# One encoder layer on one core: twelve of GpSimd's quarter sums in the first token block, probabilities transposed ahead of the weighing, first values loaded through GpSimd

## The chip, the cores and the metric

The kernel runs on one core of a Trainium2 chip. The core has a matrix engine (TensorE, PE in the profile; PEld is its weight load), VectorE (DVE), ScalarE (ACT), GpSimd (POOL) and SyncE (SP), which only issues transfers and handles semaphores. All engines run their own instruction streams and meet at semaphores. The metric is device time of one execution in microseconds, from launch to end.

## The reference, cut to what matters

One layer over 2560 tokens (a prompt of 2048 and a sample of 512), model width 1024, float32. The order of the computation is the order of the kernel:

```
h = rmsnorm(x, norm1_w)
proj = h @ w_in                       # q, k, v, z, xBC, dt
q = rmsnorm(q) * 64 ** -0.5;  k = rmsnorm(k)          # per head of 64
s = q . k_window + bias               # window of 8 rows x 16 columns on a grid 64 wide
p = softmax(s);  att = p @ v_window   # 8 heads
xBC = silu(depthwise_conv(xBC, 5 taps))
ssm = state-space mixer(z, xBC, dt)   # forward and backward scan
x = x + concat(att, ssm) @ w_out
x = x + (silu(h2 @ w_gate) * (h2 @ w_up)) @ w_down    # h2 = rmsnorm(x)
```

## The kernel before, in words

Six phases run one after the other, with a barrier of all engines between them: the input projection (tiles named i_), the attention (a_), the state-space mixer (s_), the output projection (o_), the upward (u_) and the downward (d_) half of the feed-forward part. The change touches the first two.

**Matrix products** are made of three passes over numbers split into a high and a low part (lines 65 to 67), so each weight tile i_raw becomes i_w_hi (ScalarE, L332) and i_w_lo (VectorE, L460).

**Input projection.** Five token blocks of 512 tokens each go through twelve slots s = 0 to 11 of weights. Slots 0 to 3 make xBC, 4 and 5 make z, 6 and 7 make v, 8 and 9 make q, 10 and 11 make k. Four accumulators acc[:, u] hold the four rows of 128 tokens. TensorE may start an accumulator again only when the last result in it has been taken: in slot 8 it waits for the copy of v by VectorE (L524), in slot 10 for q. The result q is scaled by VectorE (L509) and then multiplied in place by its gain by GpSimd (L630), and only GpSimd's multiplication raises the semaphore ev_ready that slot 10 waits for. At the end of a block GpSimd also makes three of the four low parts of the next block's input (L570); VectorE makes the fourth (L480). TensorE transposes the next block's input in slots 8, 9, 10 and 11 (L662).

The depthwise convolution of one token block runs a block later, in slots 4 to 7: ScalarE does the first tap (L370), VectorE the four others (L492, named taps here). In the first block (number 0) there is no earlier block, so it has no taps. The last block (number 4) does its own taps and those of block 3.

Beside this, GpSimd prepares operands for the feed-forward part, 33 of them: it loads four quarters of a weight matrix into i_ops (two transfers of 512 KB), forms four sums or differences in four instructions (L604, L605, L607, L609, and the same on L612 to L617 for the last eleven), and stores 1 MB (L620). These are the quarter sums. i_ops has two buffers: before sum n is made, the load for n + 1 is issued, and that load waits until the store of sum n - 1 has landed:

```
for n in range(OPS * tb, min(OPS * (tb + 1), 3 * FP)):
    if n + 1 < 3 * FP:
        load_ops(n + 1)
    make_ops(n)
for u in range(TT):
    pool.wait_ge(q_scaled[u], tb + 1)
    ...                               # L630, the gain of q
```

OPS is 7 and FP is 11, so blocks 0 to 3 do seven sums each and block 4 does five. In GpSimd's order they all stand ahead of the gain of q of their block.

**Attention.** Eight heads, each in 20 tiles a of 128 queries, with 3, 4, 4, 3 and 2 groups of 128 keys in the five bands of four tiles. In step a each engine does work for several tiles: TensorE makes the scores of tile a (L1143, L1144), weighs the values of tile a - 3 (L1164) and transposes the probabilities of tile a - 2 (L1152). VectorE adds the bias and takes the maximum of tile a (L964), inverts the sum of a - 1 (L979) and scales the probabilities of a - 1 if a - 1 is even (L984); GpSimd scales them if it is odd (L906). ScalarE copies the transposed probabilities of a - 2 out to a_probT (L1066), which has two buffers, and then takes the exponential of a (L1059). The q and k of the following head are prepared in between: split by ScalarE (L1039, L1040) and GpSimd (L897, L900), transposed by TensorE (L1114 to L1123), copied out by VectorE and ScalarE. At the start of the phase the same preparation is done for head 0 alone, GpSimd issues the loads of four mask blocks (L927, 480 KB each), and SP issues, in this order: q and k of head 0 in five groups, the bias of head 0 (8 transfers), the values of head 0 (L865, 16 transfers of 80 KB), then q and k (L851, L852), bias and values of head 1.

Of the kernel before, what the change touches and what calls it, by code (L numbers as in the profile page):

```python
# [23 lines left out]
HEAD = 64  # L24
# [45 lines left out]
def in_proj_phase(nc, x, w_in, cols, qk_w, bias_pad, copies, ident_dram, w_ffn, w_down, q_s, k_s, v_s, z_s, dtT, xbcT, xcT,  # L70
# [19 lines left out]
    HALO = D_CONV // 2  # L90
    CB = 4
    LAST_CONVS = (3, 3, 2, 2, 3, 1, 2, 0)
    OPS = 7

    with ExitStack() as ctx:
        def sb(name, shape, dt=F32):
# [469 lines left out]
        def _(pool):  # L566
# [53 lines left out]
                pool.dma_start(dst, ops[:, buf, 4:8]).then_inc(ops_stored[buf], 16)  # L620

            def token_block(tb, more, conv):
                for n in range(OPS * tb, min(OPS * (tb + 1), 3 * FP)):
                    if n + 1 < 3 * FP:
                        load_ops(n + 1)
                    make_ops(n)
                for u in range(TT):
                    pool.wait_ge(q_scaled[u], tb + 1)
                    view = ev[:, u].rearrange("p (h d) -> p h d", h=HEADS)
                    pool.tensor_tensor(view, view, q_gain[:].unsqueeze(1).broadcast_to([P, HEADS, HEAD]), ALU.mult) \  # L630
                        .then_inc(ev_ready[u], 1)
                if more:
                    for u in range(TT - 1):
                        h_low(tb + 1, u)
# [79 lines left out]
def attention_phase(nc, q_s, k_s, v_s, copies, masks, ident_dram, mixT):  # L714
# [27 lines left out]
    with ExitStack() as ctx:  # L742
# [36 lines left out]
        qk_loaded = some("qk_loaded", 2)  # L779
        first_loaded = some("first_loaded", BANDS)  # L780
        v_loaded = some("v_loaded", 2)
        bias_loaded = some("bias_loaded", 2)

        hi_made = sem("hi_made")
# [57 lines left out]
        def _(sp):  # L842
# [29 lines left out]
                if g == 0:  # L872
                    sp.dma_start(ident[:], ident_dram).then_inc(const_loaded, 16)
            load_bias((0, 0))
            load_v((0, 0))
            load_qk((0, 1))
            load_bias((0, 1))
            load_v((0, 1))
# [11 lines left out]
        def _(pool):  # L890
# [18 lines left out]
            def pair(i, first, last):  # L909
                for par in range(2):  # L910
# [3 lines left out]
                    for a in range(NT):  # L914
# [3 lines left out]
                        if ahead and a in at:  # L918
                            split_low(following(head), at[a])

            for g in range(BANDS):
                split_low((0, 0), g)
                if g in (1, 3):

                    i = g // 2
                    for side, which in ((qb[i], 0), (kb[i], 1)):
                        pool.dma_start(side[MASK0:MASK0 + MASKS], masks[:, which].bitcast(F32R)) \  # L927
                            .then_inc(masks_set[i], 16)
# [179 lines left out]
        def _(pe):  # L1108
# [46 lines left out]
            def weigh(head, a):  # L1155

                G, b, c, par = NT * number(head) + a, a // COLT, a % COLT, head[1]
                if a == 0:
                    pe.wait_ge(v_loaded[par], 16 * 16 * (head[0] + 1))
                if c == 0:  # L1160
                    wait(pe, o_out, BANDS * number(head) + b)
                pe.wait_ge(p_out, G + 1)
                for j in range(COUNT[b]):
                    last = pe.matmul(ps_o[HEAD * par:HEAD * (par + 1), c], v[:, par, c * KG + FIRST[b] + j],  # L1164
                                     probT[:, a % 2, j], start=j == 0, stop=j == COUNT[b] - 1)
                last.then_inc(weighed, 1)

            def pair(i, first, last):
                for par in range(2):
                    head = (i, par)  # L1170
                    ahead = not (last and par == 1)
                    at = FIRST_GROUP_AT if first and par == 0 else GROUP_AT
                    for a in range(NT):
                        scores(head, a)
                        late = behind(head, a, LAG_PV, first)
                        if late:
                            weigh(*late)
                        late = behind(head, a, LAG_TURN, first)
                        if late:
                            turn_p(*late)  # L1180
                        if ahead and a - 2 in at:
                            turn_q(following(head), at[a - 2])
                        if ahead and a - 3 in at:
                            turn_k(following(head), at[a - 3])
# [1624 lines left out]
```

## Time and profile before

| What | Value |
|---|---|
| Median of 3 runs | 3399.82 us (3389.86 to 3411.44) |
| The profiled execution | 3394.09 us, its span 3392.3 us |
| TensorE busy | 3157.7 us, 93% |
| VectorE, ScalarE, GpSimd busy | 1968.5, 1410.6, 703.6 us |
| Granted TensorE clock, mean | 0.970 |
| Input projection | 0 to 788 us |
| Attention | 789 to 1178 us |

The span runs from the first to the last instruction; 1.8 us of the profiled time lie outside it. Times in a row of the trace count from the start of the span. A clock of 1.00 is 2.4 GHz, 0.50 is 1.2 GHz.

### The profile page before, as it was taken

The page shows a single profiled execution, that of the slowest core. Times are in us where ns is not written, and L with a number is a line of the kernel's source. Part 1 is how long each engine was busy: PE and PEld are TensorE (multiplying, and loading weights), DVE is VectorE, ACT ScalarE, POOL GpSimd, SP SyncE. Part 2 cuts the span into 40 slices and gives each one's busy share as a digit, 9 for nine tenths or more (in the row PEclk, how much of TensorE's full clock was granted, in tenths as well). Part 3 has the DMA queues.
Part 4 walks back from the last instruction along what each step waited for, and adds up shares of the span by engine and source line. Part 5 has one row for each costly group of instructions (what it writes and reads, how often), then busy time and mean ns, then how long its engine had stood idle before and what let it go on. Part 6 is the DMA issues. An engine that isn't in the chain of part 4 may idle for free. (4 is left out here: it accounts for less than half of the span.)

```text
span 3392.3 us, 47727 instructions
## 1 busy us (share of the span) xinstructions
PE 3157.7 (93%) x15896; PEld 2674.9 (79%) x15896; DVE 1968.5 (58%) x3011; ACT 1410.6 (42%) x2711; POOL 703.6 (21%) x706
## 2 busy tenths in 40 slices
PE   7999999996999868869979999999999998999999
PEld 6877877774777645658868999999999997888887
DVE  3446556374666556964446555755576664555655
ACT  3334434344676536852224333432343333434443
POOL 5353534412333235832210000000000000000000
PEclk9999999998999978989989999999999998999999
DMA  8685959577333022346765545655575556566875
GB/s 275 227 295 211 332 176 347 185 249 139 80 79 76 28 81 73 93 149 211 220 212 172 159 151 162 225 157 154 154 227 175 173 175 212 211 216 241 279 243 211
DMA packets 458543, 630.37 MB, mean 186 GB/s; under 512 B 133168, under 2 KB 271968, under 8 KB 453984
## 3 DMA queue, kind: packets, MB, share of 16 engines
q1 hardware_dynamic: 431936, 522.72, 48.8%
q0 software_dynamic: 23600, 100.80, 8.4%
q10 hardware_dynamic: 2880, 5.24, 0.4%
q8 instruction: 70, 1.15, 0.1%
q14 instruction: 57, 0.47, 0.0%
HBM read 451.45 MB, written 177.75 MB: 185 GB/s over the span
## 5 line engine op out<-in xcount | busy, mean ns | idle before, releaser
L65 PE MATMUL u_acc<-u_h_hi,u_w_hi 128*128 128x448 f32 (+1 forms) x1848 | 657.1, 356 | 25.2 <-DVE u_h_lo L2378 19.9
L66 PE MATMUL u_acc<-u_h_lo,u_w_hi 128*128 128x448 f32 (+1 forms) x1848 | 656.5, 355 | 0.0
L67 PE MATMUL u_acc<-u_h_hi,u_w_lo 128*128 128x448 f32 (+1 forms) x1848 | 656.5, 355 | 0.0
L65 PEld LDWEIGHTS u_acc<-u_h_hi,u_w_hi 128*128 128x128 f32 x1848 | 347.7, 188 | 45.2 <-DVE u_w_lo L2366 22.8
L66 PEld LDWEIGHTS u_acc<-u_h_lo,u_w_hi 128*128 128x128 f32 x1848 | 347.7, 188 | 18.4
L67 PEld LDWEIGHTS u_acc<-u_h_hi,u_w_lo 128*128 128x128 f32 x1848 | 347.6, 188 | 18.4
L2622 ACT CAST d_hi<-d_raw 128x896 fp32r<-128x896 f32 (+1 forms) x231 | 224.2, 980 | 279.8 <-DMA d_raw<-hid_ops 151.2
L460 DVE TENSOR_TENSOR i_w_lo<-i_raw,i_w_hi 128x2048 fp32r<-128x2048 f32 x60 | 155.3, 2589 | 305.6 <-ACT i_w_hi L332 305.6
L2643 DVE TENSOR_TENSOR d_lo<-d_raw,d_hi 128x896 fp32r<-128x896 f32 (+1 forms) x231 | 252.0, 1133 | 113.3 <-ACT d_hi L2622 108.4
L65 PE MATMUL d_acc<-d_hi 128*128 128x512 f32 x770 | 301.8, 392 | 17.1 <-DVE d_lo L2643 12.8
L66 PE MATMUL d_acc<-d_lo,d_hi 128*128 128x512 f32 x770 | 301.3, 391 | 0.0
L67 PE MATMUL d_acc<-d_hi,d_lo 128*128 128x512 f32 x770 | 301.3, 391 | 0.0
L65 PE MATMUL i_acc<-i_w_hi,i_h_hi 128*128 128x512 f32 x640 | 257.7, 403 | 10.4 <-DVE i_ev L524 10.4
L66 PE MATMUL i_acc<-i_w_lo,i_h_hi 128*128 128x512 f32 x640 | 255.8, 400 | 0.0
L67 PE MATMUL i_acc<-i_w_hi,i_h_lo 128*128 128x512 f32 x640 | 255.7, 400 | 0.0
L2321 ACT ACTIVATE u_gate<-u_gate 128x448 f32<-128x448 f32 (+1 forms) x99 | 55.6, 562 | 401.5 <-DVE u_gate L2421 204.9
L2366 DVE TENSOR_TENSOR u_w_lo<-u_w_lo,u_w_hi 128x512 fp32r<-128x512 f32 x264 | 180.6, 685 | 50.7 <-ACT u_w_hi L2306 43.4
L65 PEld LDWEIGHTS d_acc<-d_hi 128*128 128x128 f32 x770 | 145.7, 189 | 48.4 <-DVE d_lo L2643 13.2
L1164 PE MATMUL a_ps_o<-a_probT,a_v 128*64 128x128 f32 x1024 | 148.0, 283 | 34.2 <-ACT a_probT L1066 19.6
L332 ACT CAST i_w_hi<-i_raw 128x2048 fp32r<-128x2048 f32 x60 | 114.4, 1907 | 151.0 <-PE i_acc L67 150.3
L1164 PEld LDWEIGHTS a_ps_o<-a_probT,a_v 128*64 128x64 f32 x1024 | 109.1, 138 | 85.2 <-ACT a_probT L1066 49.1
L2306 ACT CAST u_w_hi<-u_w_lo 128x512 fp32r<-128x512 f32 x264 | 152.7, 616 | 43.5 <-DMA u_w_lo<-w_ops 43.5
(265 smaller groups left out, 6072.3 us busy)
## 6 DMA issues: line engine op xcount, KB each, us to landing
u_w_lo<-w_ops SPq DMA_DIRECT2D x264, 256.0 KB, 2.9
i_raw<-w_in_dram SPq DMA_DIRECT2D x60, 1024.0 KB, 6.5
u_w_raw<-w_ffn_dram SPq DMA_DIRECT2D x198, 256.0 KB, 3.2
d_raw<-wd_ops SPq DMA_DIRECT2D x132, 256.0 KB, 5.5
d_raw<-hid_ops SPq DMA_DIRECT2D x154, 192.0 KB, 6.1
d_raw<-w_down_dram SPq DMA_DIRECT2D x99, 256.0 KB, 5.7
i_ops<-w_ffn_dram POOLq DMA_DIRECT2D x44, 512.0 KB, 6.5
w_ops<-i_ops POOLq DMA_DIRECT2D x22, 1024.0 KB, 6.3
```

The source lines that it names most:

```text
L65: pe.matmul(out, w_hi, x_hi, start=first, stop=False, skip_group_check=resumed)
L66: pe.matmul(out, w_hi, x_lo, start=False, stop=False, skip_group_check=resumed)
L67: return pe.matmul(out, w_lo, x_hi, start=False, stop=last, skip_group_check=resumed)
L332: act.copy(w_hi[:, par], raw[:, par]).then_inc(slot_hi_done[par], 1)
L460: dve.tensor_tensor(w_lo[:, par], raw[:, par], w_hi[:, par].bitcast(F32), ALU.subtract) \
L1164: last = pe.matmul(ps_o[HEAD * par:HEAD * (par + 1), c], v[:, par, c * KG + FIRST[b] + j], probT[:, a % 2, j], start=j == 0, stop=j == COU ...
L2306: act.copy(w_hi[:, n], weights(n)).then_inc(w_hi_done, 1)
L2321: act.activation(gate[:, c, 0:n], gate[:, c, 0:n], ACT.Silu).then_inc(silu_done, 1)
L2366: dve.tensor_tensor(w_lo[:, n], weights(n), w_hi[:, n].bitcast(F32), ALU.subtract) \
L2622: act.copy(hi[:, r, 0:TB + w], raw[:, r, 0:TB + w]).then_inc(hi_done, 1)
L2643: dve.tensor_tensor(lo[:, r, 0:TB + w], raw[:, r, 0:TB + w], hi[:, r, 0:TB + w].bitcast(F32), ALU.subtract) \
```

## The change

Three edits. The table OPS_AT gives blocks 0 to 4 of the input projection 12, 5, 5, 5 and 6 sums in place of 7, 7, 7, 7 and 5; the total stays 33. The values of head 0 are issued by GpSimd, ahead of its first splits, and not by SP; they have a semaphore of their own, and the counts of the old one are lowered for even heads. In each attention step the transposition of tile a - 2 stands ahead of the weighing of tile a - 3.

```diff
-    OPS = 7
+    OPS_AT = (0, 12, 17, 22, 27, 33)
...
             def token_block(tb, more, conv):
-                for n in range(OPS * tb, min(OPS * (tb + 1), 3 * FP)):
+                for n in range(OPS_AT[tb], OPS_AT[tb + 1]):
                     if n + 1 < 3 * FP:
                         load_ops(n + 1)
                     make_ops(n)
...
+        first_v_loaded = sem("first_v_loaded")
...
             load_bias((0, 0))
-            load_v((0, 0))
             load_qk((0, 1))
...
+            v_src = v_s.rearrange("(m r c) d -> r c m d", r=4, c=GRID_W)
+            for c in range(COLT):
+                for r in range(4):
+                    pool.dma_start(v[32 * r:32 * r + 32, 0, c * KG:(c + 1) * KG], v_src[r, COL[c]:COL[c] + 32, :, 0:HEAD]) \
+                        .then_inc(first_v_loaded, 16)
             for g in range(BANDS):
                 split_low((0, 0), g)
...
                 if a == 0:
-                    pe.wait_ge(v_loaded[par], 16 * 16 * (head[0] + 1))
+                    if isinstance(head[0], int) and head == (0, 0):
+                        pe.wait_ge(first_v_loaded, 16 * 16)
+                    else:
+                        pe.wait_ge(v_loaded[par], 16 * 16 * (head[0] + par))
...
                         scores(head, a)
+                        late = behind(head, a, LAG_TURN, first)
+                        if late:
+                            turn_p(*late)
                         late = behind(head, a, LAG_PV, first)
                         if late:
                             weigh(*late)
-                        late = behind(head, a, LAG_TURN, first)
-                        if late:
-                            turn_p(*late)
```

GpSimd at the end of block 0 of the input projection, before: one quarter sum (the seventh), then the gain of q and the low parts.

```order
L604 TENSOR_TENSOR i_ops<-i_ops 128x512
L605 TENSOR_TENSOR i_ops<-i_ops 128x512
L607 TENSOR_TENSOR i_ops<-i_ops 128x512
L609 TENSOR_TENSOR i_ops<-i_ops 128x512
L620 DMA w_ops<-i_ops 128x2048
L630 TENSOR_TENSOR i_ev<-i_ev,i_q_gain 128x512 x4
L570 TENSOR_TENSOR i_h_lo<-i_h_f,i_h_hi 128x8x128 x3
```

The same place as a difference; the first of the five sums that are added is shown, and the four others stand between it and the gain of q.

```order
 L609 TENSOR_TENSOR i_ops<-i_ops 128x512
 L620 DMA w_ops<-i_ops 128x2048
+L577 DMA i_ops<-w_ffn_dram 128x1024
+L579 DMA i_ops<-w_ffn_dram 128x1024
+L604 TENSOR_TENSOR i_ops<-i_ops 128x512
+L605 TENSOR_TENSOR i_ops<-i_ops 128x512
+L607 TENSOR_TENSOR i_ops<-i_ops 128x512
+L609 TENSOR_TENSOR i_ops<-i_ops 128x512
+L620 DMA w_ops<-i_ops 128x2048
```

Five such groups of seven rows now stand ahead of L630 and L570 of block 0 on GpSimd.

TensorE in an attention step with four groups of keys, before.

```order
L1143 MATMUL a_ps_s<-a_ka,a_qa 128x512
L1144 MATMUL a_ps_s<-a_kb,a_qb 128x512
L1164 MATMUL a_ps_o<-a_probT,a_v 64x128 x4
L1152 MATMUL a_ps_p<-a_ident,a_prob 128x128 x4
```

And the same step now (the line numbers are those of the changed kernel; L1148 and L1149 are the scores, L1157 the transposition, L1172 the weighing).

```order
L1148 MATMUL a_ps_s<-a_ka,a_qa 128x512
L1149 MATMUL a_ps_s<-a_kb,a_qb 128x512
L1157 MATMUL a_ps_p<-a_ident,a_prob 128x128 x4
L1172 MATMUL a_ps_o<-a_probT,a_v 64x128 x4
```

The last two groups have changed places, and so have the waits in front of them.

GpSimd at the start of the attention, now; before, the first row was not there.

```order
L924 DMA a_v<-v_s 32x10x64 x16
L897 TENSOR_TENSOR a_q_st<-a_q_raw,a_q_st 128x4x64
L900 TENSOR_TENSOR a_k_st<-a_k_raw,a_k_st 128x4x64
L897 TENSOR_TENSOR a_q_st<-a_q_raw,a_q_st 128x4x64
L900 TENSOR_TENSOR a_k_st<-a_k_raw,a_k_st 128x4x64
L932 DMA a_qb<-masks_dram 48x2560
L932 DMA a_kb<-masks_dram 48x2560
```

All of GpSimd's work of the start, the splits that TensorE waits for and the mask loads, now stands behind the sixteen issues.

## Rows read from the trace of the kernel before

**Rows 1.** The page: the span.

```profile
span 3392.3 us, 47727 instructions
```

**Rows 2.** Time line of GpSimd, block 0: start us, us, what, [idle before <-releaser].

```profile
93.18 0.53 POOL L577 DMA_DIRECT2D i_ops<-w_ffn_dram  x1 [3.89 <-DMA w_ops<-i_ops]
...
108.74 0.53 POOL L577 DMA_DIRECT2D i_ops<-w_ffn_dram  x1 [8.45 <-DMA w_ops<-i_ops]
...
120.13 0.53 POOL L577 DMA_DIRECT2D i_ops<-w_ffn_dram  x1 [4.26 <-DMA w_ops<-i_ops]
...
126.67 0.58 POOL L620 DMA_DIRECT2D w_ops<-i_ops  x1 [0.30 <-POOL i_ops L609]
143.29 1.28 POOL L630 TENSOR_TENSOR i_ev<-i_ev,i_q_gain 128x512 f32<-128x512 f32 x1 [16.04 <-DVE i_ev L509]
```

**Rows 3.** Time line of TensorE: the transposition between slots 9 and 10 of block 0.

```profile
146.70 1.03 PE L662 MATMUL i_ps_turn<-i_ident,i_x_t 128*128 128x128 f32 x8
```

**Rows 4.** Time line of TensorE: the first matmul of slot 8, blocks 1 to 3.

```profile
276.72 0.77 PE L65 MATMUL i_acc<-i_w_hi,i_h_hi 128*128 128x512 f32 x1 [3.53 <-DVE i_ev L524]
...
431.02 0.77 PE L65 MATMUL i_acc<-i_w_hi,i_h_hi 128*128 128x512 f32 x1 [4.05 <-DVE i_ev L524]
...
585.93 0.47 PE L65 MATMUL i_acc<-i_w_hi,i_h_hi 128*128 128x512 f32 x1 [2.29 <-DVE i_ev L524]
```

**Rows 5.** Busy time by stretch; the last three columns: PEclk, DMA share, GB/s.

```profile
431.00:437.00 6.00, 5.98 (x15) 4.71 (x16) 6.00 (x8) 1.74 (x3) 0.00 (x0) 0.52 0.84 289
...
586.00:592.00 6.00, 6.00 (x20) 4.76 (x20) 6.00 (x8) 2.48 (x5) 0.00 (x0) 0.72 0.84 290
...
640.00:646.00 6.00, 6.00 (x18) 4.73 (x17) 3.59 (x3) 1.95 (x2) 5.87 (x4) 0.58 0.62 232
```

**Rows 6.** Time line of VectorE, the taps of block 1.

```profile
246.66 10.15 DVE L492 SCALAR_TENSOR_TENSOR i_cy<-i_cx,i_cols,i_cy 128x512 f32<-128x512 f32 x8 [0.42 <-ACT i_cy L370]
...
258.93 5.38 DVE L492 SCALAR_TENSOR_TENSOR i_cy<-i_cx,i_cols,i_cy 128x512 f32<-128x512 f32 x8
...
266.43 9.55 DVE L492 SCALAR_TENSOR_TENSOR i_cy<-i_cx,i_cols,i_cy 128x512 f32<-128x512 f32 x8
```

**Rows 7.** Time line of GpSimd beside them: end of the fifth sum, an add.

```profile
239.80 0.58 POOL L620 DMA_DIRECT2D w_ops<-i_ops  x1 [0.30 <-POOL i_ops L609]
...
262.76 4.92 POOL L604 TENSOR_TENSOR i_ops<-i_ops 128x512 f32<-128x512 f32 x1
```

**Rows 8.** Time line of TensorE, start of the attention: first scores, first two weighings.

```profile
808.53 0.42 PE L1143 MATMUL a_ps_s<-a_ka,a_qa 128*128 128x384 f32 x1 [1.34 <-ACT a_qb L1047]
...
820.57 1.54 PE L1164 MATMUL a_ps_o<-a_probT,a_v 128*64 128x128 f32 x6 [8.14 <-DMA a_v<-v_s]
...
828.81 1.54 PE L1164 MATMUL a_ps_o<-a_probT,a_v 128*64 128x128 f32 x6 [5.01 <-ACT a_probT L1066]
```

**Rows 9.** Time line of GpSimd at the attention's start: its first split.

```profile
793.45 0.72 POOL L897 TENSOR_TENSOR a_q_st<-a_q_raw,a_q_st 128x256 fp32r<-128x256 f32 x1 [28.32 <-ACT a_k_st L1040]
```

**Rows 10.** Time line of SP's queue: issue of the values of head 0.

```profile
799.60 18.45 SPq L865 DMA_DIRECT2D a_v<-v_s  x16
```

**Rows 11.** Groups of GpSimd: transfers that it issues, count, busy us and mean ns.

```profile
L644 POOL DMA_DIRECT2D bias_copies<-rpb_dram x16 | 8.0, 509 | 0.0
L640 POOL DMA_DIRECT2D xbcT<-i_zero x3 | 2.8, 948 | 0.4 <-POOL i_zero L636 0.4
```

**Rows 12.** Transfers from 780 to 850 us.

```profile
DMA packets 31670, 10.49 MB, mean 150 GB/s; under 512 B 30832, under 2 KB 30960, under 8 KB 31472
```

**Rows 13.** Waits from 832 to 1178 us: engine line <- waited for: us, times, longest.

```profile
PE a_ps_o L1164 <- ACT a_probT L1066: 13.7, 52, 0.5
PE a_ps_o L1164 <- DVE a_outT L995: 4.8, 7, 0.8
```

**Rows 14.** Time line of one attention step: GpSimd's scaling, then TensorE.

```profile
840.53 1.04 POOL L906 TENSOR_TENSOR a_prob<-a_prob,a_inv 128x512 f32<-128x512 f32 x1 [2.34 <-DVE a_inv L979]
...
842.12 1.09 PE L1164 MATMUL a_ps_o<-a_probT,a_v 128*64 128x128 f32 x8
```

## The prediction

> **What bounds the kernel now.** I began with the page: TensorE is busy for 93% of the span of 3392.3 us [rows 1], so only a stretch in which TensorE waits can be shortened, and any new wait of TensorE counts in full. I then took TensorE's waits phase by phase, and for each wait the time line of the engine that ends it. In the input projection TensorE has three waits for VectorE's copy of v, one in each of the blocks 1 to 3 [rows 4]; in block 0 it runs through from its first matmul to the edge of the block. At the start of the attention it waits 8.14 us for the values of head 0 and 5.01 us for a copy of probabilities that stands behind a late load on ScalarE [rows 8]. In the steady attention it waits in 59 places for 18.5 us in all, before the weighing [rows 13]. These are all the waits that the change can touch. Nothing of it reaches the later phases.
>
> **The sums in block 0.** Here the reader should look at who gives slot 10 its accumulators. Slot 10 of TensorE starts when slot 9 and a transposition are done, at 146.70 + 0.8 = 147.5 us [rows 3]. It needs GpSimd's gain of q, which was made at 143.29, after 16.04 us of idleness [rows 2]. That gap is GpSimd's slack: with the 4.2 us by which TensorE comes later, some 20 us. Five more sums now stand ahead of the gain. A sum takes about 5.2 us of adds, but its period is longer, since each load waits until the last store has landed. From one load to the next it was 120.13 - 108.74 = 11.4 us where the store landed 4.26 us after its issue ended, and 108.74 - 93.18 = 15.6 us where it took 8.45 [rows 2]. Between 8.5 and 4 us I take 6 for the store issued at 126.67, so the eighth sum's load goes out at 133.2. The eighth follows at the mixed pace of 13 us, and from then on TensorE stands, its weight loads stop, and nothing but these transfers is under way, so the others go at the 11.4 pace: the twelfth sum's load goes out near 133.2 + 13 + 3 x 11.4 = 180.4. From a load to the end of the following store's issue it is 126.67 + 0.58 - 120.13 = 7.1 us, and the first gain takes 1.3: slot 10 starts at 188.8, in place of 147.5. **That is 41 us lost.** At the fast pace throughout it is 133.2 - 2 + 4 x 11.4 + 8.4 - 147.5 = 37.7 us; at 15.6 throughout, from 135.7, it is 59. Queued behind the late gains on GpSimd are the low parts of block 1, which are needed two slots later and keep their distance, and on SP's queue the stores of q with the next block's weights, which have those two slots too.
>
> After 2.76 us of idleness at the edge of block 4 the granted clock was 0.58 over the next six microseconds, near the lower of its levels, 1.2 GHz in place of 2.4 [rows 5]. That is 2.5 us of full speed lost. I add it once for the restart of slot 10, 0 to 3 as bounds. **Block 0: +43.5.**
>
> **The sums in blocks 1 to 3.** Eight taps take 5.38 us on VectorE alone and 10.15 or 9.55 with GpSimd's adds beside them, and one of GpSimd's adds, 1.3 us elsewhere, took 4.92 while the unhindered taps ran [rows 6, 7]. The fifth sum of block 1 ends at 239.80 [rows 7], before the taps at 246.66, so with five sums a block two groups of taps are freed: 4.8 + 4.2 = 9 us of VectorE's time, ahead of a copy that is 3.53 us late. The same two sums fall away in blocks 2 and 3, with 4.05 and 2.29 us to be won. I take all of it, 9.9 us [rows 4]; the first group of taps of each block stays contended and is absorbed. The clock, too, had fallen after these waits: 0.52 over six microseconds after the second and 0.72 after the third [rows 5], which gives back 2.9 + 1.7 = 4.6 us. **Together -14.5**, with -9.9 and -16 as bounds. Block 4 has one sum more, at the start of its taps; that costs VectorE 0 to 4.8 us by the same rows, and gives nothing back. TensorE is not held by VectorE alone there. I take +1.
>
> **The values of head 0 on GpSimd.** Removed is SP's issue of 18.45 us [rows 10], so q and k of head 1 go out at 799.6 and no longer at 818, and the wait of 5.01 us behind them should go with the 8.14 for the values themselves. Added are sixteen issues ahead of GpSimd's first split, which ran at 793.45 [rows 9]. The trace has no such transfer on GpSimd. The bounds are 0.51 us each, for short plain copies, and 0.95, for transfers of 1024 short runs; these have 320 runs of 256 bytes, so I take 0.6 [rows 11]. From 789.4 this ends at 799.0 (797.6 and 804.6 by the bounds), so the first split is 5.6 us later (4.1 to 11.1), and the first scores come at 814. The masks, which the scores need as well, now follow the values on GpSimd's queue. Ahead of and with them are q, k, bias, values and two masks of head 0, 4.0 MB; at the 150 GB/s of this stretch [rows 12] these are there 27 us after 789.4, at 816.4. I take that. TensorE was ready to weigh 820.57 - 8.14 - 808.53 = 3.9 us after the first scores and ready for the second weighing 3.2 us later [rows 8], so the second weighing comes at 823.5 in place of 828.81. **-6**, with -13 (both waits gone, nothing delayed) and +4 as bounds, the latter from the rival below.
>
> A rule of the Trainium skill speaks against this edit. "Trainium Kernel Development and Optimization", section Key Constraints, says that transfers issued from SP, ScalarE and GpSimd run on the same 16 DMA engines, so that issuing from several of them only saves the sequencer's issue time. By it neither of the two waits need go, and the sum would be 10 us larger; no row here shows whether it holds for these transfers. The rival on bandwidth says what that would look like here.
>
> **The order in the step.** The weighing waits for a copy of probabilities that ScalarE can only begin when the transposition is done; before, the next scores alone covered that copy. Now a whole step lies between, and the waits of 13.7 and 4.8 us, the latter for VectorE's copy of the output, should vanish [rows 13]. What is late next is the transposition: it needs the scaled probabilities and had the weighing, 1.1 us, as cover. GpSimd's scaling ended at 841.57 and the transposition would now begin at 842.12, so 0.55 us are left [rows 14]. In the bands with two or three groups the steps are shorter and the margin is smaller; I grant new waits of 0.1 us in half of the 160 tiles, 7.5 us. **-11**; bounds -18.5 and +13.5, the latter from the rival below.
>
> **The sum.** 43.5 - 14.5 + 1 - 6 - 11 = +13. Against the profiled execution, 3394.1 us with 1.8 of it outside the span, that is 3407. The median of the runs is 5.7 us above the profiled one, so I predict 3413. Three runs of one kernel lay 22 us apart, so about 1%, 34 us, is what a measurement of this kernel can tell from no change.
>
> **Rivals.** *GpSimd's scaling becomes the bound of the step.* It is the mechanism on the slow side. If each of the 80 odd tiles keeps TensorE waiting 0.4 us, which is what the 1.04 us of one scaling against a margin of 0.55 would give, that is +32 - 18.5 = +13.5 in place of -11: 3437, over 1% slower. It passes 1% from new waits above some 0.35 us per odd tile. For it speaks that GpSimd also makes the splits of the following head; against it, that the exponential comes earlier too, since ScalarE no longer waits for the late transposition. 8%.
>
> *The stores stay slow.* If the sums in block 0 keep the 15.6 pace, the stall is 59: 3431. Against it speaks that TensorE's weight loads stop during the stall. 12%.
>
> *The start is bound by bandwidth.* If also q, k and bias of head 1, 1.7 MB, come between the masks' bytes, 5.7 MB at 150 GB/s end 38 us after 789.4, at 827.4, the first scores stand at that time, and the second weighing comes at 834.5: +6 in place of -6, held to +4 since less is left to load afterwards. 3423. For it speaks that 30832 of the 31670 packets of this stretch are under 512 bytes [rows 12]. 10%.
>
> *No stall in block 0.* If the five sums fitted into the slack of 20 us, or slot 10 did not need the gain, the 43.5 fall out: 3369. Each sum would have to take 4 us, and its four adds alone take 5.2; so this is the case in which I have misread the wait. 5%.
>
> **How the numbers follow.** The forecast has 65%. The range must reach the slow stores and most of the slow side, and on the fast side a stall of 38 with the larger gains of the attention, some 25 us under the forecast: 3388 to 3438. The case over 1% faster needs the last rival, with nothing lost elsewhere: 5%. Over 1% slower is the first rival with half of the slow stores' case, where both add up: 13%. The rest is 82%.
>
> **What the changed profile would show.** One wait of TensorE of 38 to 47 us in slot 10 of block 0, ended by GpSimd's L630; no waits for L524 in blocks 1 to 3, and taps of 5.4 us in the second, third and fourth group; first scores at 814 to 817 after the start of the phase is set to 789.4, no wait for the values; no waits for the copy of probabilities, and new short ones of L1157 for the scaling. The prediction is wrong above all if the first is missing or has another size: it is worth more than everything else together.

## The result, and the profile after

The changed kernel takes 3435.91 us (median of 4 runs, 3413.37 to 3447.35). The kernel before, run beside it, takes 3404.49 (4 runs, 3389.86 to 3411.44). The ratio is 1.0077, 95% interval 1.004 to 1.0114: slower, by some 0.8%. The forecast was 3413, range 3388 to 3438.

The two profiled executions tell where the time went, if one cuts them at events that both have: the first matmul of each block and the last of the input projection, the second and the last weighing, and the first matmul of the output projection. Each number is the distance between two such rows of TensorE's time line.

| Stretch, us | before | after | difference | predicted |
|---|---|---|---|---|
| input projection, block 0 | 149.3 | 194.8 | +45.5 | +43.5 |
| blocks 1 to 3 | 464.0 | 447.0 | -17.0 | -14.5 |
| block 4 | 143.7 | 150.6 | +6.9 | +1 |
| last matmul to second weighing | 46.2 | 46.3 | +0.1 | -6 |
| second weighing to last weighing | 353.1 | 345.3 | -7.8 | -11 |
| mixer, whose code is the same | 316.4 | 325.4 | +9.0 | 0 |

The first five differ by +27.7 in sum, +13 was predicted, and the medians differ by 31. The mixer's 9 us come up below; its code is the same in both kernels.

The span, which answers to [rows 1]:

```profile
span 3427.8 us, 47729 instructions
```

**Block 0.** GpSimd's time line, from the seventh sum on; the columns are start, duration, what, and in brackets the idle time ahead and what ended it. It answers to [rows 2]; the load at 171.30 is left out.

```profile
119.75 0.53 POOL L577 DMA_DIRECT2D i_ops<-w_ffn_dram  x1 [4.24 <-DMA w_ops<-i_ops]
...
132.43 0.53 POOL L577 DMA_DIRECT2D i_ops<-w_ffn_dram  x1 [5.57 <-DMA w_ops<-i_ops]
...
147.62 0.53 POOL L577 DMA_DIRECT2D i_ops<-w_ffn_dram  x1 [6.16 <-DMA w_ops<-i_ops]
...
160.43 0.53 POOL L577 DMA_DIRECT2D i_ops<-w_ffn_dram  x1 [3.88 <-DMA w_ops<-i_ops]
...
182.17 0.53 POOL L577 DMA_DIRECT2D i_ops<-w_ffn_dram  x1 [3.88 <-DMA w_ops<-i_ops]
...
188.57 0.58 POOL L620 DMA_DIRECT2D w_ops<-i_ops  x1 [0.30 <-POOL i_ops L609]
189.17 4.97 POOL L630 TENSOR_TENSOR i_ev<-i_ev,i_q_gain 128x512 f32<-128x512 f32 x4
```

Five sums stand ahead of the gain of q, and the gain no longer waits for anything: GpSimd itself is late. The distances between the loads are 12.7 and 15.2 us while TensorE works, then 12.8 and twice 10.9 when it stands and little but these transfers is under way. TensorE's time line shows the other end of it, beside [rows 3]:

```profile
146.23 1.03 PE L662 MATMUL i_ps_turn<-i_ident,i_x_t 128*128 128x128 f32 x8
...
190.58 0.77 PE L65 MATMUL i_acc<-i_w_hi,i_h_hi 128*128 128x512 f32 x1 [43.32 <-POOL i_ev L630]
...
744.97 0.47 PE L65 MATMUL i_acc<-i_w_hi,i_h_hi 128*128 128x512 f32 x1 [2.64 <-ACT i_ev L419]
...
771.92 0.47 PE L65 MATMUL i_acc<-i_w_hi,i_h_hi 128*128 128x512 f32 x1 [2.71 <-DVE i_ev L524]
```

**Blocks 1 to 4.** The waits of [rows 4] are gone: between 221 and 740 us TensorE waits only at the edges of blocks, where it waited before too. VectorE's taps in block 1, for instance, take 10.26 us in the first group, where GpSimd's fifth sum still runs, and 5.4 in the others, of which the first is shown; [rows 6] had two slow ones out of three.

```profile
281.01 10.26 DVE L492 SCALAR_TENSOR_TENSOR i_cy<-i_cx,i_cols,i_cy 128x512 f32<-128x512 f32 x8 [3.29 <-ACT i_cy L370]
293.89 5.44 DVE L492 SCALAR_TENSOR_TENSOR i_cy<-i_cx,i_cols,i_cy 128x512 f32<-128x512 f32 x8 [0.42 <-ACT i_cy L370]
...
727.00 14.13 DVE L492 SCALAR_TENSOR_TENSOR i_cy<-i_cx,i_cols,i_cy 128x512 f32<-128x512 f32 x12
```

The last row is block 4. Twelve taps take 14.13 us there beside the sixth sum. The two waits of TensorE in block 4, above, are its consequence. VectorE's copy of v comes late, as it did in the other blocks before. It had been late in block 4 as well, by 0.50 us, a wait that [rows 4] leave out:

```profile
737.82 0.47 PE L65 MATMUL i_acc<-i_w_hi,i_h_hi 128*128 128x512 f32 x1 [0.50 <-DVE i_ev L524]
```

ScalarE's copy of z (L419) stands behind activations that waited for these taps:

```profile
739.84 1.96 ACT L377 ACTIVATE i_co<-i_cy 128x512 f32<-128x512 f32 x3 [5.45 <-DVE i_cy L492]
741.70 2.50 ACT L370 ACTIVATE i_cy<-i_cx,i_cols 128x512 f32<-128x512 f32 x3
744.22 2.07 ACT L419 ACTIVATE i_ev<-i_acc 128x512 f32<-128x512 f32 x4
```

Read by stretch, one for each block (us, busy time and number of instructions of PE, PEld, DVE, ACT and POOL; then granted clock, DMA share, GB/s), the same shows as busy time of VectorE. First blocks 1 and 4 of the kernel before, then blocks 0, 1 and 4 of the changed one. At the same number of VectorE's instructions, block 1 went from 86.47 to 80.33 us and block 4 from 84.95 to 90.17.

```profile
174.92:329.79 154.87, 148.33 (x632) 119.06 (x633) 86.47 (x74) 59.51 (x81) 68.82 (x57) 0.97 0.72 258
...
638.93:782.60 143.67, 143.17 (x599) 114.81 (x600) 84.95 (x95) 60.93 (x81) 40.45 (x35) 0.98 0.67 233
...
25.90:220.72 194.82, 148.50 (x632) 119.37 (x633) 58.01 (x41) 46.81 (x62) 109.34 (x110) 0.88 0.69 247
220.72:369.48 148.76, 145.71 (x632) 117.09 (x633) 80.33 (x74) 58.94 (x81) 50.03 (x43) 0.99 0.69 241
...
667.69:818.30 150.61, 145.26 (x600) 116.05 (x600) 90.17 (x95) 61.24 (x81) 47.98 (x42) 0.97 0.66 236
```

**Start of the attention.** GpSimd issues the sixteen transfers in 9.53 us, 0.60 each, ahead of its first split. ScalarE then waits for the keys of head 1, and behind that wait stands a copy of probabilities (L1071) for which TensorE waits before its second weighing. The first row answers to [rows 9], those of TensorE to [rows 8]; the time lines are of GpSimd, TensorE, ScalarE and SP.

```profile
825.53 9.53 POOL L924 DMA_DIRECT2D a_v<-v_s  x16 [24.78 <-POOLq L58]
835.08 0.74 POOL L897 TENSOR_TENSOR a_q_st<-a_q_raw,a_q_st 128x256 fp32r<-128x256 f32 x1
...
850.86 0.45 PE L1148 MATMUL a_ps_s<-a_ka,a_qa 128*128 128x384 f32 x1 [1.59 <-DMA a_kb<-masks_dram]
...
856.16 1.54 PE L1172 MATMUL a_ps_o<-a_probT,a_v 128*64 128x128 f32 x6
864.58 1.54 PE L1172 MATMUL a_ps_o<-a_probT,a_v 128*64 128x128 f32 x6 [5.40 <-ACT a_probT L1071]
...
863.23 0.40 ACT L1044 CAST a_q_st<-a_q_raw 128x256 fp32r<-128x256 f32 x1 [7.33 <-DMA a_k_raw<-k_s]
...
825.01 0.39 SPq L871 DMA_DIRECT2D a_q_raw<-q_s  x1
...
838.32 0.98 SPq L852 DMA_DIRECT2D a_q_raw<-q_s  x1
839.34 11.32 SPq L853 DMA_DIRECT2D a_k_raw<-k_s  x1
```

From SP's first load of q (789.37 before, 825.01 after) the first scores stand at 19.2 before and 25.9 after, the first weighing at 31.2 and 31.1, the second at 39.4 and 39.6. The wait for the values has gone, and the scores have come later by nearly as much. SP comes to the load of the keys of head 1 some 15 us earlier in this count (14.3 us after the first load in place of 29.6), and not the 18 us of the values' issue, since the bias ahead of it took longer too. It then needs 11.32 us for that one instruction, where it needed 2.16 before. ScalarE has the keys 38.1 us after the first load before and 38.2 after.

**Steady attention.** TensorE's waits from 867 to 1210 us (engine, line, what it waited for; us, times, longest), to be held against [rows 13]. Those stop some 3 us short of the last weighing, which stands at 1181.9 us; up to it the kernel before waits 14.6 us in 54 places for the copy.

```profile
PE a_ps_p L1157 <- POOL a_prob L906: 2.9, 12, 0.4
PE a_ps_o L1172 <- DVE a_outT L1000: 1.6, 6, 0.3
PE a_ps_o L1172 <- ACT a_probT L1071: 0.9, 2, 0.5
```

The waits for the copy of probabilities are 2, and GpSimd's scaling is late in 12 of some 80 odd tiles, by 0.24 us each.

### The profile page after: what moved, and what is told of

The parts are those of the page before. It is cut to its first block and busy times, and to the rows that moved or that the text cites. A ratio compares the mean times of both kernels' runs of the same rounds, so it can differ in the third digit from the quotient of the medians.

```text
span 3427.8 us, 47729 instructions
## 1 busy us (share of the span) xinstructions
PE 3168.5 (92%) x15896; PEld 2681.8 (78%) x15896; DVE 1954.6 (57%) x3011; ACT 1418.6 (41%) x2711; POOL 699.2 (20%) x722
## 5 line engine op out<-in xcount | busy, mean ns | idle before, releaser
L460 DVE TENSOR_TENSOR i_w_lo<-i_raw,i_w_hi 128x2048 fp32r<-128x2048 f32 x60 | 162.5, 2708 | 348.4 <-ACT i_w_hi L332 348.3
L65 PE MATMUL i_acc<-i_w_hi,i_h_hi 128*128 128x512 f32 x640 | 257.7, 403 | 48.8 <-POOL i_ev L630 43.3
L2374 DVE TENSOR_TENSOR u_w_lo<-u_w_lo,u_w_hi 128x512 fp32r<-128x512 f32 x264 | 180.5, 685 | 50.8 <-ACT u_w_hi L2314 43.5
L332 ACT CAST i_w_hi<-i_raw 128x2048 fp32r<-128x2048 f32 x60 | 114.5, 1908 | 188.8 <-PE i_acc L67 182.8
L65 PEld LDWEIGHTS i_acc<-i_w_hi,i_h_hi 128*128 128x128 f32 x640 | 121.9, 191 | 79.2 <-issue 50.2
L67 PEld LDWEIGHTS d_acc<-d_hi,d_lo 128*128 128x128 f32 x770 | 144.9, 188 | 30.4
```

What stands on the lines that cost most here:

```text
L65: pe.matmul(out, w_hi, x_hi, start=first, stop=False, skip_group_check=resumed)
L67: return pe.matmul(out, w_lo, x_hi, start=False, stop=last, skip_group_check=resumed)
L332: act.copy(w_hi[:, par], raw[:, par]).then_inc(slot_hi_done[par], 1)
L460: dve.tensor_tensor(w_lo[:, par], raw[:, par], w_hi[:, par].bitcast(F32), ALU.subtract) \
L2374: dve.tensor_tensor(w_lo[:, n], weights(n), w_hi[:, n].bitcast(F32), ALU.subtract) \
```

## The experiments

Each ratio is against the kernel before, run beside it on the same chip. Its median was 3407.58 us (29 runs) beside the three single parts and the eight sums, 3407.47 (29 runs) beside the moved masks, the moved gain and the first kernel of the last section, and 3409.64 (12 runs) beside the two others.

### Each part alone

**The table alone** (first), **the order of the step alone** (second), **the values of head 0 alone** (third):

```diff
-    OPS = 7
+    OPS_AT = (0, 12, 17, 22, 27, 33)
```

```diff
                         scores(head, a)
-                        late = behind(head, a, LAG_PV, first)
-                        if late:
-                            weigh(*late)
                         late = behind(head, a, LAG_TURN, first)
                         if late:
                             turn_p(*late)
+                        late = behind(head, a, LAG_PV, first)
+                        if late:
+                            weigh(*late)
```

```diff
-            load_v((0, 0))
...
+            v_src = v_s.rearrange("(m r c) d -> r c m d", r=4, c=GRID_W)
+            for c in range(COLT):
+                for r in range(4):
+                    pool.dma_start(v[32 * r:32 * r + 32, 0, c * KG:(c + 1) * KG], v_src[r, COL[c]:COL[c] + 32, :, 0:HEAD]) \
+                        .then_inc(first_v_loaded, 16)
```

> The kernel before with the table of sums alone (12, 5, 5, 5, 6). My theory: the gain of q, which stands behind the twelve sums on GpSimd, keeps TensorE waiting 43 us in slot 10 of block 0; the taps of blocks 1 to 3 are freed and give 17 back, the sixth sum of block 4 costs 7. Sum: 35 us slower than before (ratio 1.010), the last matmul of the input projection near 817. Rival: the whole change lost its time elsewhere, in the mixer phase, which took 9 us more in the profile of the changed kernel; then this kernel is 26 us slower or less in the runs.

> The kernel before with the transposition ahead of the weighing alone. My theory: TensorE's visible waits in the steady attention fall from 18.5 us to about 5, and the time from the second weighing to the last shrinks by 8 us; ratio 0.997. Rival: GpSimd's scaling becomes the bound, new waits of 0.4 us in each odd tile: 5 to 13 us slower, ratio 1.002 to 1.004.

> The kernel before with the values of head 0 on GpSimd alone. Theory A, bandwidth: the wait for the values (8 us) goes, the scores come 6 to 7 us later, and the wait for k of head 1 stays, so that the second weighing stands where it stood, 39.4 us after the phase's first transfer; ratio 1.000. Theory B, issue time: with k of head 1 issued 18 us earlier the second weighing comes some 6 us earlier; ratio 0.998.

The table alone: 3442.48 us, ratio 1.0129 (1.009 to 1.0169). TensorE's time line repeats that of the whole change, one row for each of its three new waits:

```profile
190.50 0.77 PE L65 MATMUL i_acc<-i_w_hi,i_h_hi 128*128 128x512 f32 x1 [43.31 <-POOL i_ev L630]
...
744.80 0.47 PE L65 MATMUL i_acc<-i_w_hi,i_h_hi 128*128 128x512 f32 x1 [2.42 <-ACT i_ev L419]
...
771.99 0.47 PE L65 MATMUL i_acc<-i_w_hi,i_h_hi 128*128 128x512 f32 x1 [2.93 <-DVE i_ev L524]
```

Its input projection ends at 818.3 as well, 35.7 us later than before, and the medians are 34.9 us apart. Its mixer took 315.0 us in the profile, against 316.4 before, so the rival, a loss in that phase, is not needed. The table alone is the loss.

The order of the step alone: 3399.1 us, ratio 0.999 (0.9955 to 1.0024). The ratio doesn't tell it from nothing, but the stretch from the first scores to the last weighing falls from 373.4 to 367.0 us in the profile, and the steady waits fall to 2.8, 1.6 and 0.9 us. In the profiles it gives 6 to 8 us.

The values alone: 3414.48 us, ratio 1.0035 (1.0008 to 1.0062). First scores 25.4 us after SP's first load, weighings at 29.6 and 39.3:

```profile
810.76 0.45 PE L1148 MATMUL a_ps_s<-a_ka,a_qa 128*128 128x384 f32 x1 [1.38 <-DMA a_kb<-masks_dram]
...
824.64 1.54 PE L1172 MATMUL a_ps_o<-a_probT,a_v 128*64 128x128 f32 x6 [6.64 <-ACT a_probT L1071]
```

The second weighing stands where it stood. No gain, with the order of the step untouched: the missing 6 us are this edit's own. The small loss that the ratio shows is not in this stretch of the profile. In this execution the mixer took 330.1 us in place of 316.4; whether the edit has a part in that is not shown.

### Eight sums in block 0

```diff
-    OPS = 7
+    OPS_AT = (0, 8, 14, 20, 26, 33)
```

> The kernel before with the table 8, 6, 6, 6, 7. My theory: the eighth sum of block 0 ends at 141.5, ahead of the gain of q, so there is no wait of TensorE in slot 10; with six sums in blocks 1 to 3 one of two contended groups of taps is freed (4 to 5 us of VectorE's time), which covers the waits of 3.5 and 2.3 us and most of the 4.1: 8 to 14 us won with the clock; seven sums in block 4 cost 7 to 15. Sum: between 6 us faster and 7 us slower, ratio 0.998 to 1.002. Rival: any sum more in block 0 costs TensorE its whole period: 13 us in slot 10.

It took 3406.93 us, ratio 0.9998 (0.9971 to 1.0025). GpSimd's time line of block 0 and then TensorE's of block 4:

```profile
141.43 0.58 POOL L620 DMA_DIRECT2D w_ops<-i_ops  x1 [0.30 <-POOL i_ops L609]
143.34 1.28 POOL L630 TENSOR_TENSOR i_ev<-i_ev,i_q_gain 128x512 f32<-128x512 f32 x1 [1.33 <-DVE i_ev L509]
...
712.29 0.79 PE L65 MATMUL i_acc<-i_w_hi,i_h_hi 128*128 128x512 f32 x1 [2.86 <-DVE i_w_lo L460]
...
730.81 0.76 PE L65 MATMUL i_acc<-i_w_hi,i_h_hi 128*128 128x512 f32 x1 [5.54 <-DVE i_ev L524]
```

The eighth sum ends 1.33 us before VectorE has q ready, so it costs block 0 nothing, and the gain is made at 143.34 against 143.29 in [rows 2]. By that the slack of 20 us that I read from the gap holds one sum of 13 us and not two. Blocks 1 to 3 take 148.6, 149.8 and 148.8 us with six sums each, as fast as with five. Block 4, with seven, takes 155.9 us and has given 12 of the 17 us back.

### Is the start bound by bytes

If the second pair of mask blocks (480 KB each) stands ahead of the keys of head 1 only as bytes on the same transfer engines, moving it to step 6 of head 0 must bring these keys some 6 us earlier, whoever issues the values. That is theory A below. The first of two kernels leaves the values on SP, the second has them on GpSimd:

```diff
+            def load_masks(i):
+                for side, which in ((qb[i], 0), (kb[i], 1)):
+                    pool.dma_start(side[MASK0:MASK0 + MASKS], masks[:, which].bitcast(F32R)) \
+                        .then_inc(masks_set[i], 16)
...
+                        if first and par == 0 and a == 6:
+                            load_masks(1)
...
-                if g in (1, 3):
...
+                if g == 1:
+                    load_masks(0)
```

> The kernel before, with the second pair of mask loads (960 KB, needed only by head 1) issued by GpSimd in step 6 of head 0 and no longer at the start of the phase. Theory A, bandwidth: the bytes that go ahead of the values and of k of head 1 shrink by 1 of some 6 MB, and the second weighing comes 4 to 6 us earlier than 39.4 us after the phase's first transfer; ratio 0.9985. Theory B, issue time: the second weighing stands at 39 us.

> The values of head 0 on GpSimd, and the second pair of mask loads issued in step 6 of head 0. Theory A, bandwidth: the second weighing, at 39.3 us after the phase's first transfer with the values on GpSimd alone, comes 4 to 6 us earlier. Theory B, issue time: the first scores stay at 25.9 us and the second weighing at 39.

The first took 3404.95 us, ratio 1.0002 (0.9972 to 1.0032); SP's first load is at 788.04. TensorE's time line, then a row of ScalarE's and one of SP's:

```profile
813.14 1.54 PE L1167 MATMUL a_ps_o<-a_probT,a_v 128*64 128x128 f32 x6 [1.42 <-DMA a_v<-v_s]
821.37 1.54 PE L1167 MATMUL a_ps_o<-a_probT,a_v 128*64 128x128 f32 x6 [5.00 <-ACT a_probT L1069]
...
820.01 0.40 ACT L1042 CAST a_q_st<-a_q_raw 128x256 fp32r<-128x256 f32 x1 [7.82 <-DMA a_k_raw<-k_s]
...
798.52 12.06 SPq L865 DMA_DIRECT2D a_v<-v_s  x16
```

The weighings come 25.1 and 33.3 us after the first load, where they came 31.2 and 39.4: both 6.1 us earlier. SP issues the same sixteen transfers in 12.06 us in place of 18.45 [rows 10]. Nothing of SP's work was changed, so at least these 6.4 us of its issue time were a wait for what stood ahead on the transfer engines.

The second took 3407.41 us, ratio 1.0008 (0.9975 to 1.0041); SP's first load is at 785.59:

```profile
810.89 0.44 PE L1151 MATMUL a_ps_s<-a_ka,a_qa 128*128 128x384 f32 x1 [1.34 <-DMA a_kb<-masks_dram]
...
818.63 1.54 PE L1175 MATMUL a_ps_o<-a_probT,a_v 128*64 128x128 f32 x6
...
817.28 0.40 ACT L1047 CAST a_q_st<-a_q_raw 128x256 fp32r<-128x256 f32 x1 [1.36 <-DMA a_k_raw<-k_s]
```

ScalarE has the keys 31.7 us after the first load, as in the first kernel (32.0) and not 37.9 to 38.2 as in the three kernels with four mask blocks ahead. The four kernels make a table of two by two: the masks move the keys by 6.1 and 6.2 us, and the issuing engine moves them by 0.3 at most, which is less than the six further profiles with four mask blocks ahead differ among each other (38.0 to 38.8). The second weighing, at 33.0, is no earlier than in the first kernel, because the scores still come at 25.3, behind GpSimd's sixteen issues and its mask.

The runs don't show these 6 us: both ratios are 1 within their intervals, which are some 10 us to either side. That the start is shorter rests on the profiles.

### The gain of q after the eighth sum

The twelve sums of block 0 stay, but the gain is made after the eighth and the four others follow it, ahead of the low parts of the next block.

```diff
+    SPLIT = ((8, 0, 4), (5, 0, 0), (5, 0, 0), (5, 0, 0), (6, 0, 0))
...
+                sums(at, before_v)
...                                       # the gain of q
+                sums(at + before_v + before_q, after_q)
```

> The table 12, 5, 5, 5, 6 alone, but in block 0 the gain of q stands behind the eighth sum, with four sums between the gain and the low parts. My theory, the order on GpSimd: the wait in slot 10 is gone, and TensorE waits at the edge of block 0 instead, for the low parts behind the twelfth sum: block 1 starts at 205 to 213 in place of 175 (220.7 with all twelve ahead of the gain). Rival, the stall is the contention of the extra sums with VectorE: a wait of some size stays in slot 10.

One run, 3434.25 us. Slot 10 has no wait, and TensorE's time line has this at the edge of block 1:

```profile
205.77 0.77 PE L65 MATMUL i_acc<-i_h_hi,i_w_hi 128*128 128x512 f32 x1 [33.80 <-POOL i_h_lo L571]
```

The low parts of the next block are needed two slots later, and GpSimd now comes to them at 198.59. Block 1 starts 15 us earlier than with the gain last, since TensorE does its two last slots beside the four sums, which rules out the rival, a wait in slot 10 from contention; the 33.8 us that these don't cover are waited for at the next place. What block 0 can't hold is the time of four sums, in either of the two orders tried.

### Block 4 with five sums

```diff
-    OPS_AT = (0, 12, 17, 22, 27, 33)
+    OPS_AT = (0, 12, 17, 22, 28, 33)
```

> The table 12, 5, 5, 6, 5 alone: one sum less in block 4, one more in block 3. Theory (the sixth sum of block 4, beside the first groups of its taps, cost that block what it lost): block 4 takes 143.7 us as before, in place of 150.6, and its waits for the copy of v and for ScalarE's copy of z are gone; block 3 stays within 1 us of 149.6, since its six sums end ahead of its taps' second group. Rival (block 4 lost its time because it now begins in another state, with the sums of the blocks ahead moved): it stays near 150. The wait of 43 us in block 0 is as it was.

One run, 3431.11 us. The input projection ends at 807.6 and not at 818.3, and of the two waits in block 4 that for L419 is gone and that for L524 is 1.27 us, in slot 8, where the kernel before waited 0.50. The expectation had both gone. TensorE's row and all of block 4, columns as above:

```profile
762.77 0.47 PE L65 MATMUL i_acc<-i_w_hi,i_h_hi 128*128 128x512 f32 x1 [1.27 <-DVE i_ev L524]
...
664.31:807.60 143.29, 142.02 (x600) 113.87 (x600) 81.95 (x95) 60.94 (x81) 38.92 (x35) 0.99 0.66 233
```

Block 3, with six sums, takes 664.31 - 515.77 = 148.5 us; it pays nothing for the sixth. Block 4 takes 143.3. Over all the profiles, one of each kernel, block 4 gives a series. With five sums it took 141.2 to 145.8 us in six kernels (143.7 before, 143.3 here), with six 150.0 to 150.6 in three, with seven 155.9, and with three, in the two kernels of the next section, 142.5 and 143.8. The sixth sum costs some 7 us and the seventh 5; taking away two of the five gives nothing that stands out of their spread. This run has the sums of the other blocks moved as well, and its block 4 is as short as before, so the rival is ruled out.

### A version that uses what was found

Thirty-three sums where they cost nothing: nine in block 0, of which eight ahead of the gain and one behind it; seven in blocks 1 to 3, of which five at the start, one after VectorE has copied v and one after the gain; three in block 4. With it the changed order of the step, the values on SP. The second kernel also moves the second pair of masks.

```diff
+    SPLIT = ((8, 0, 1), (5, 1, 1), (5, 1, 1), (5, 1, 1), (3, 0, 0))
+    OPS_AT = (0, 9, 16, 23, 30, 33)
...
+                sums(at, before_v)
+                if before_q:
+                    pool.wait_ge(ev_ready[TT - 1], tb * USES + USE[6] + 1)
+                    sums(at + before_v, before_q)
```

> The transposition ahead of the weighing, the values back on SP, and the sums spread: block 0 makes eight ahead of the gain of q and one between the gain and the low parts; blocks 1 to 3 make five, one more after VectorE's copy of v, and one between the gain and the low parts; block 4 makes three. My theory: no wait of TensorE in slot 10 of block 0, none for the copy of v in blocks 1 to 4; blocks of 148.5 us in place of 154.9, 155.5 and 153.7, the last 0.5 us shorter: 18 us won in the input projection, and 8 by the order of the step: 26 us faster, ratio 0.992. Rival: a sum between the gain and the low parts delays the low parts, and each of four block edges loses up to 5 us: ratio 0.998.

> The kernel of the run before that spread the sums and changed the order of the step, with the second pair of mask blocks issued in step 6 of head 0 in place of the start of the phase. Theory (the bytes queued at the start of the attention set the two waits): the first weighing loses 6 us of its wait for the values, the second stays 5 us after it, so 6 us more are gained: ratio against the kernel before near 0.992, some 3380 us. Rival (the gains don't add, since the later masks collide with the changed order of the step or the time comes back in the mixer): ratio 0.9943 or above, as without the masks moved.

The first took 3385.88 us (12 runs), ratio 0.9943 (0.9915 to 0.997). Its input projection ends at 763.1 us, 19.5 before that of the kernel before, with these waits of TensorE from 30 us on:

```profile
PE i_acc L65 <- DVE i_h_lo L481: 11.6, 4, 3.0
PE i_acc L65 <- DVE i_ev L525: 0.4, 1, 0.4
```

The second took 3378.02 us (7 runs), ratio 0.9907 (0.9872 to 0.9941). The intervals of the two overlap, so the runs alone don't show that the masks add something; the profile does, since the attention from first scores to last weighing is 361.8 us against 368.6. Both are faster than the kernel before and than the changed one.

## Why the prediction was nearly right, and where not

**Block 0: right, +45.5 for +43.5.** The wait is one, in slot 10, ended by L630, and 43.3 us long against 41. The load ahead of the eighth sum went out at 132.43 (133.2 in the sum), that ahead of the twelfth at 182.17 (180.4), and slot 10 started at 190.58 (188.8). The pace was 15.2 us once where I had 13, and 10.9 us at the end where I had 11.4. The rival of slow stores, 15.6 throughout, did not come. The restart was sized well too: the granted clock was 0.50, the lower level, over the first 6 us from 190.58 on, and from the start of slot 10 to the edge of the block it took 30.1 us in place of 27.4, for the 2.5 of the sum. The eighth sum alone, in the run with eight, confirms the slack, and the run with the gain moved shows that it is mostly GpSimd's time and not the order.

**Blocks 1 to 3: right, -17.0 for -14.5**, one microsecond beyond the bound of 16. All three waits went, and the runs with six sums a block went as fast. The clock gave back more than the 4.6 us that the two stretches of [rows 5] showed: its mean over the three blocks went from 0.97 to between 0.98 and 0.99.

**Block 4: the size was wrong, +6.9 for +1, beyond the bound of 4.8.** The step that failed is "TensorE is not held by VectorE alone there. I take +1". I had priced the sum by what it adds to one group of taps and taken the rest as slack. But TensorE was held by VectorE there: [rows 4] and the prediction's count of three waits leave out a fourth, of 0.50 us for L524 in block 4, shown above. Block 4 does two blocks' worth of taps and has no slack for a sixth sum. The run with five sums there has 143.3 us, and the series shows some 7 us for the sixth and 5 for the seventh. The wait that I didn't look for was ScalarE's copy of z, queued behind an activation that waits for the taps.

**The values of head 0: wrong, 0 for -6, inside its bounds.** The step that failed is that q and k of head 1, ordered earlier, would also be there earlier, so that "the wait of 5.01 us behind them should go". They landed 38.2 us after the first load in place of 38.1. That is the rival on bandwidth in kind, and the profiles with the masks moved show it: 6.2 us for the bytes, 0.3 at most for the issuer. Its end of the bytes, 38 us after the first load, was right. Its +4 to +6 was too much because it let the first scores wait for all of these bytes; they came at 25.9 us, and only the keys, and with them the second weighing, came at the end. By the section Key Constraints of "Trainium Kernel Development and Optimization" in the Trainium skill, which the prediction set against this edit, transfers from the three issuing engines share the same 16 DMA engines and only the issue time is saved. The trace agrees in what it says of the keys, which landed no earlier; the wait for the values itself, 8.14 us, did go, against scores that came 6.7 us later. The first term of the same part, 0.6 us for each issue, measured 0.60, the first split came 6.0 us later for 5.6, and the first scores at 815.3, if the phase is set to begin at 789.4, for 816.4. Two slips of the working don't decide anything: 828.81 - 823.5 is 5.3 and not 6, and 0.1 us in half of 160 tiles is 8 and not 7.5.

**The order of the step: right in kind, -7.8 for -11.** The waits of [rows 13], 18.5 us, became 5.4 with their successors. Of the 13.1 us fewer only 7.8 were gained. The remainder is not idle time elsewhere: from the second weighing to the last TensorE's busy time rose from 328.4 to 335.8 us at the same matmuls and the same granted clock, 0.99. Why a wait that goes comes back in part as busy time is not shown. The new waits for GpSimd's scaling are 2.9 us in 12 places for the 7.5 in 80 that I had granted. So this rival is ruled out, alone and with the rest.

**The rest: +9 in the mixer is not traced to the change.** The mixer's code is the same in all kernels here, and its time went from 315 to 339 us between the profiled executions, of which there is one for each kernel: 316.4 before, 315.0 with the table alone, 325.4 after, 338.3 and 338.7 in the two of the last section, which are the fastest kernels. Two stretches of the same work show what differs (columns as above; the third from the end is the granted clock, 1.00 being 2.4 GHz). They begin some 150 us after the phase does, when TensorE had issued 553 and 558 of its matmuls. In the kernel before:

```profile
1334.00:1384.00 50.00, 44.39 (x312) 32.26 (x310) 46.17 (x53) 39.96 (x154) 39.41 (x30) 1.00 0.28 81
```

In the first kernel of the last section:

```profile
1310.00:1360.00 50.00, 44.70 (x260) 32.57 (x260) 39.40 (x48) 33.62 (x129) 31.66 (x25) 0.84 0.27 79
```

TensorE issues 260 matmuls in place of 312 in 50 us, at a granted clock of 0.84 in place of 1.00, and the other engines do as much less. What decides which of the two an execution gets stays open: no run was made for it. That the work ahead of the phase has a part is not ruled out, since the two kernels of the last section, which share their sums and the order of the step, have nearly the same mixer. The medians speak against a fixed cost of that size: the first of the two gained 19.5 + 4.8 = 24.3 us in the stretches that its edits touch and 21.6 in the medians, although its mixer took 22 us longer in the profile. The change's 9 us are below what the medians of four runs each can tell.

A sum of terms therefore has to be held against the stretches that the change touches. There it is +27.7 for +13, and the 14.7 between them are block 4 (5.9), the values (6.1), the order of the step (3.2) and block 0 (2.0), less 2.5 in blocks 1 to 3. The forecast of the median was 23 us low. These 14.7 explain most of it, and 4.7 more are that the kernel before took 3404.49 us beside the change and not 3399.82. The result lies 2 us inside the range, and that is in part luck: the upper side of the range was there for slow stores and late scaling, neither of which came, and the misses on block 4 and the values used it up.

## What to carry to other kernels

Moving side work to a block that "has nothing to do" is a matter of how long it takes there, from load to load and not in busy time: the gap of 16 us held one sum, the four beyond it cost 43 us of the busiest engine, and another order on the same queue moved most of that wait to the next consumer. Before an engine is blamed for issuing loads slowly, ask what bytes stand ahead of it: an issue of 18.45 us shrank to 12.06 when another engine's load was taken away, and giving the issue to another engine gained nothing. And a short wait is a sign that the slack is used up: TensorE waited 0.50 us for VectorE's copy in block 4, and one sum more there cost 7.

## What the runs showed of the hardware

- SP's issue of the keys of head 1, one transfer of 640 KB, took 11.32 us in the changed kernel, where that of q just ahead took 0.98, and 2.16 in the kernel before, behind the values.
- GpSimd's issue of a transfer of 320 runs of 256 bytes took 0.60 us, between the 0.51 and 0.95 of [rows 11].
- GpSimd's fourth add of a sum took 3.20 us in place of 1.26 in one sum of the stall, and in the sum before it 3.23, so adds are held up also where no taps run. Both adds ended within 0.02 us of VectorE's L474, at 155.7 and 140.6 us, and VectorE's L460 beside them took 4.42 and 3.11 us, where it takes 2.29 alone.
- The granted clock in the mixer, from 150 us after its begin, in stretches of 50 us, was 0.83 to 0.86 in the two profiled executions of the last section and 0.90 to 1.00 before, after and with the table alone, at the same work. TensorE was busy for 0.89 of the two stretches shown.
